# Begin the inverse with the score tiles, and put the panel split and the rotary angles ahead of it

## The reference, cut to what matters

```python
def step(state, inp):
    r_t, w_t, k_t, v_t, kk_t, a_t = inp
    sa = jnp.einsum('bhvk,bhk->bhv', state, -kk_t)
    state = (state * w_t[:, :, None, :] + sa[..., None] * (kk_t * a_t)[:, :, None, :]
             + v_t[..., None] * k_t[:, :, None, :])
    return state, jnp.einsum('bhvk,bhk->bhv', state, r_t)
```

## Time and profile before

| what | value |
|---|---|
| median of 3 runs | 1281.81 us (1281.0 to 1282.97) |
| the profiled execution | 1281.0 us, its span 1278.7 us |
| TensorE busy | 1133.4 us, 89% of the span |
| VectorE busy | 642.2 us, 50% |
| ScalarE busy | 467.8 us, 37% |
| mean granted TensorE clock | 0.959 |

### The profile page before, as it was taken

The page is one execution under the profiler, slowest core; times in us unless marked ns, Lnnn a source line. Parts: engine busy times, 40 slices in busy tenths (PEclk is TensorE's granted clock), DMA queues, the critical chain, the costliest instruction groups (busy, mean ns, idle before and its releaser), DMA issues.

```text
span 1278.7 us, 18185 instructions
## 1 busy us (share of the span) xinstructions
PE 1133.4 (89%) x7641; PEld 911.9 (71%) x7641; DVE 642.2 (50%) x899; ACT 467.8 (37%) x566; POOL 24.8 (2%) x43
## 2 busy tenths in 40 slices
PE   2599999999999989699688988795999999999985
PEld 2588757778887677587466766584888888878864
DVE  4867556355343456953853537635453333342334
ACT  4422441323323446555335655316312222232222
POOL 0100000000000000000000001000000000000000
PEclk9999989999999889899889999897999999999988
DMA  7866423311014331137031144722353322222201
GB/s 265 260 217 223 146 82 100 111 44 43 19 44 152 129 124 56 45 108 266 8 114 41 45 144 157 256 84 83 132 165 99 99 99 90 96 78 99 99 1 66
DMA packets 105401, 143.40 MB, mean 112 GB/s; under 512 B 3028, under 2 KB 86088, under 8 KB 105320
## 3 DMA queue, kind: packets, MB, share of 16 engines
q1 hardware_dynamic: 91816, 105.76, 25.3%
q0 software_dynamic: 6016, 22.84, 5.1%
q10 hardware_dynamic: 7488, 13.63, 2.9%
HBM read 126.50 MB, written 15.73 MB: 111 GB/s over the span
## 4 chain that ended last, share of the span: by engine, by line
PE 70%; DVE 16%; ACT 10%; issue 2%; DMA 1%; ACTq 0%; DVEq 0%; SPq 0%; POOL 0%
PE bank L1804 69%; DVE wlo L1175 2%; ACT whi L764 2%; DVE ada_acc L1178 2%; DVE mg L1175 1%; DMA raw<-in_ada_w 1%; ACT gate_row L779 1%; DVE q_lev L1175 1%; DVE Z L1175 1%; ACT sg L1131 1%; DVE near L1585 1%; DVE k_lev L1175 1%; DVE x L1175 1%; ACT x_norm L792 1%; ACT LX L887 1%
## 5 line engine op out<-in xcount | busy, mean ns | idle before, releaser
L1804 PE MATMUL bank<-hhi,whi 128*128 128x512 f32 x816 | 333.1, 408 | 11.8 <-DVE wlo L1175 8.9
L1175 DVE TENSOR_TENSOR wlo<-raw,whi 128x2048 fp32r<-128x2048 f32 (+1 forms) x82 | 175.2, 2136 | 333.8 <-ACT whi L764 333.1
L1804 PE MATMUL bank<-hlo,whi 128*128 128x512 f32 x816 | 323.3, 396 | 0.0
L1804 PE MATMUL bank<-hhi,wlo 128*128 128x512 f32 x816 | 322.8, 396 | 0.0
L764 ACT ACTIVATE whi<-raw 128x2048 fp32r<-128x2048 f32 (+1 forms) x82 | 146.9, 1792 | 220.7 <-PE bank L1804 205.0
L1804 PEld LDWEIGHTS bank<-hhi,whi 128*128 128x128 f32 x816 | 156.7, 192 | 55.4 <-DVE wlo L1175 9.6
L1804 PEld LDWEIGHTS bank<-hhi,wlo 128*128 128x128 f32 x816 | 156.4, 192 | 34.2
L1804 PEld LDWEIGHTS bank<-hlo,whi 128*128 128x128 f32 x816 | 157.1, 193 | 31.5 <-issue 0.5
L1804 PE MATMUL bank<-whi,d_hi 128*128 128x512 f32 x176 | 70.4, 400 | 7.7 <-DVE d_lo L1175 7.7
L1804 PE MATMUL bank<-wlo,d_hi 128*128 128x512 f32 x176 | 70.0, 398 | 0.0
L1804 PE MATMUL bank<-whi,d_lo 128*128 128x512 f32 x176 | 69.9, 397 | 0.0
(11 more groups left out here) (314 smaller groups left out, 1543.4 us busy)
## 6 DMA issues: line engine op xcount, KB each, us to landing
raw<-in_w_in SPq DMA_DIRECT2D x33, 1024.0 KB, 5.5
raw<-in_ada_w SPq DMA_DIRECT2D x24, 1024.0 KB, 5.2
raw<-in_f_in SPq DMA_DIRECT2D x22, 1024.0 KB, 5.1
early_out<-gate_row ACTq DMA_DIRECT2D x52, 256.0 KB, 2.0
raw<-in_f_out SPq DMA_DIRECT2D x11, 1024.0 KB, 4.9
sg<-early_out POOLq DMA_DIRECT2D x4, 1536.0 KB, 9.8
raw<-in_w_out SPq DMA_DIRECT2D x4, 1024.0 KB, 8.3
x_in<-in_x POOLq DMA_DIRECT2D x4, 512.0 KB, 7.9
```

Of the source, the lines that this page charges most:

```text
L1175: return v.tensor_tensor(out_, a, b, op)
L1804: return t.matmul(out_, lhsT, rhs, start=start, stop=stop, skip_group_check=True)
```

## The change

TensorE computes the four "rw sc" tiles before the two "rw n" tiles, and the bank plan adds them in that order. ScalarE takes "rw n" after early("rw pro") and after early(("rw lo", c)) instead of before. VectorE runs early("rw pro") ahead of begin_inverse(0), and in the rounds begin_inverse(c + 1) after the angles and the dot products instead of before them.

```diff
     def inverse_start(n):
         b.add("rw v", n)
-        for g in range(2):
-            b.add("rw n", n, g)
         for ab in range(2):
             for g in range(2):
                 b.add("rw sc", n, ab, g)
+        for g in range(2):
+            b.add("rw n", n, g)
...
             take_values(0)
+            early("rw pro")
             take_first(0)
-            early("rw pro")
...
                 take_values(c + 1)
+                early(("rw lo", c))
                 take_first(c + 1)
-                early(("rw lo", c))
                 take_r(c, 0)
...
+            early("rw pro")
             begin_inverse(0)
-            early("rw pro")
...
             for c in range(PAIRS - 1):
-                begin_inverse(c + 1)
                 if c == 0:
                     angles(1)
                 elif c == 1:
...
+                begin_inverse(c + 1)
                 early(("rw lo", c))
...
                 end(last, "rw v", n)
+                for ab in range(2):
+                    ps = [begin("rw sc", n, ab, g) for g in range(2)]
+                    for hl in range(4):
+                        for g in range(2):
+                            last = mm(ps[g][:, P * hl:P * hl + P], rows64(BK, g, hl, 2 * n + ab), rows64(AR, g, hl, 2 * n + ab))
+                            if hl == 3:
+                                end(last, "rw sc", n, ab, g)
                 ps = [begin("rw n", n, g) for g in range(2)]
...
-                for ab in range(2):
-                    ps = [begin("rw sc", n, ab, g) for g in range(2)]
...
```

## The result

The changed kernel took 1301.13 us (median of 4 runs, 1297.88 to 1302.47) against 1281.85 us for the kernel before (4 runs, 1281.0 to 1282.97). The ratio is 1.0146, interval 1.0125 to 1.0168. It was timed again later: 1302.88 against 1281.42 us, ratio 1.0157 (1.0137 to 1.0177). The forecast was 1304.2 us, slower by 22.4; measured was 19.3 and, the second time, 21.5 slower. The profiled execution of the changed kernel took 1297.93 us, at the lower end of its runs.

What follows compares the result with a forecast made beforehand. TensorE was taken to bound the kernel, so its stalls add to the end time. 8.2 + 3.8 + 3.8 + 0 + 6.6 = +22.4 us on the 1281.81 us median gave 1304.2 us; range 1296.5 to 1308.5.

Steps and rivals of the forecast that it cites:

- The wait of n for the masks: Ahead of the rounds n waits for VectorE's masks, +8.2 us; rounds 0 and 1, behind angles, +3.8 us net each.
- That the bank is the cause: In the inverse's start, n takes banks of the first two sc tiles, so it waits until VectorE masks them.
- the wait moves to `X`: Rival: n's bank is free, TensorE stops only at level 1; +10.3 us in all, 1292.1 us, chance 0.06.
- What the rounds get back: Rounds 0 and 1: TensorE's wait for `X` at level 1 goes, giving back 0.7 us of 4.5 in each.
- Round 2: Last inverse begun, no angles ahead of the masks: cost 0, up to 1.9 us if ScalarE's cover were gone.
- The clock: Behind each of three TensorE gaps, ahead of the rounds and in rounds 0 and 1: 2.2 us, 6.6 in all.
- stalls without the clock: Rival: the same three gaps come but the clock costs nothing; +15.8 us, 1297.6 us, chance 0.10.
- Sum: Whole kernel: 8.2 + 3.8 + 3.8 + 0 + 6.6 = +22.4 us, 1304.2 us.
- the shift at the stage's end stays to the end of the kernel: Profile sign: about 22 us later at the end of the stage, unchanged to the end of the kernel.
- Given back entirely: Rival: the stage ends later, but what it delays waits for something else anyway; 1281.8 us, chance 0.04.
- faster: Rival: in all four places masks start up to 1.0 us sooner, removing TensorE waits; -4.7 us, 1277.1 us, chance 0.05.

Runs made afterwards that it cites:

- TensorE's order alone: Kernel before with only TensorE's order and the bank plan changed, sc ahead of n; 1282.27 us (1.0004).
- gaps filled: Changed kernel plus matmuls nobody reads between sc and n, 32 ahead of the rounds, 17 in each of rounds 0 and 1; 1296.88 us (1.0113).
- TensorE undone: Changed kernel with TensorE's order and the bank plan as before, VectorE's and ScalarE's moves kept; 1296.06 us (1.0111).
- version to beat both: Kernel before with angles between levels 3 and 4, values in their own bank, and ScalarE copying n before the values; 1277.68 us (0.9969).
- n in other banks: Changed kernel with the two n tiles in banks 4 and 5, which VectorE need not free; 1289.92 us (1.0062).
- VectorE undone: Changed kernel with both of VectorE's edits taken back, TensorE's and ScalarE's kept; 1278.13 us (0.9978).
- angles undone: Changed kernel with begin_inverse(c + 1) ahead of the angles again in the rounds; 1288.12 us (1.0048).
- angles in the middle: Kernel before with only the angles and lambda moved between levels 3 and 4; 1277.85 us (0.9979).
- first begin undone: Changed kernel with VectorE running begin_inverse(0) before early("rw pro") again; 1287.88 us (1.0050).

## Why the prediction was right

- *The wait of n for the masks.* Right in mechanism and size. Ahead of the rounds I had 8.1 to 8.2 us; the run with filled gaps has 7.8 without the clock. In the rounds I had 3.8 net; 3.7 each. The gaps were 7.69, 4.38 and 4.42 us. The 0.4 us too much ahead of the rounds is ScalarE: its second store took 0.33 us in the queue, and the high half started at 231.40, not 231.83.
- *That the bank is the cause* was argued from the bank plan; giving n other banks showed it. The rival "the wait moves to `X`", priced at 5.1, 1.5 and 1.5 us and 2.2 for the clock behind the first, is what that kernel does: 7.5, 1.5 and 1.5, less 0.4 in round 2.
- *What the rounds get back.* I said that the wait for `X` is there once; it is there in rounds 0 and 1, 1.4 us in all, and was priced in both. I let the two waits go because the angles move. They go by TensorE's order alone as well, as three runs show; the number was right, the credit too narrow.
- *Round 2.* 0 forecast, -0.4 measured. The reason for no cost held: `LX` is copied by 374.63, and VectorE comes to it at 375.18.
- *The clock.* 2.2 us for each gap forecast, 6.6 in all; 2.7, 2.3 and 2.1 in the first profile, 1.5, 1.7 and 1.7 in the second. The rival "stalls without the clock" fell: filling the gaps took 6.7 us out of the stage. So the size was right in the first profile, and 1.6 us too high in the second; which of the two an execution gets was not foreseeable from the rows. By the 0.62, 0.67 and 0.71 above, 8 us x 2 x (1 - clock) is 6.1, 5.3 and 4.6 us at half clock. The Trainium skill (TensorE: Matmul & The Clock Gate, Terms) puts the penalty at the throttled time times (1 - K/N), half of it at half clock; that would be an estimate of 3.0, 2.6 and 2.3 us. The runs have 0.2 to 0.3 us less in each.
- *Sum.* +22.4 forecast, +22.0 and +19.8 in the stage, +19.3 and +21.5 in the medians. The term that was missing is outside the stage: I said that the shift at the stage's end stays to the end of the kernel, and 5.0 and 1.8 us of it came back behind it as the clock fell for less time there. That was neither priced nor in the range's reasoning. That the second difference of the medians comes within 1 us of the forecast is in part luck: in its profile 2.1 us less than in the first in the stage and 1.8 given back stand against 3.9 us lost ahead of the stage, which the edit doesn't touch.
- *Given back entirely* and *faster* fell with the result. The latter's mechanism was real, though: with VectorE's edits undone the rest of the change is worth 1.6 us in the stage.

What comes back behind the stage is the clock's. The 13 profiles differ in how long it stands at half around two places there, 421 and 462 us in the kernel before (read in windows of 0.2 us), and the time from the stage's end to the end of the kernel follows it:

| at half clock at the two places | profiles | from the stage's end to the last instruction |
|---|---|---|
| 13.6 us | kernel before (both), gaps filled, TensorE undone, version to beat both | 895.7 to 896.6 us |
| 10.2 us | changed kernel (second), n in other banks, VectorE undone | 894.3 to 894.8 us |
| 6.8 us | angles undone, TensorE's order alone, angles in the middle | 893.3 to 893.6 us |
| 3.4 us | changed kernel (first), first begin undone | 891.6 us |

Open: what decides between these. It is not the length of the stage, since versions with a longer and with a shorter one stand in the same row; the kernel before shows the same stretches twice and the changed kernel does not, and no run separates a cause in the order of the program from chance.

## What to carry to other kernels

When tiles share banks in rotation, exchanging two of them also exchanges whose reader they wait for; look up who frees the bank, and what stands ahead of that release in its reader's queue. Here, 5.5 us of angles moved ahead of a release made waits of 4.4 us, and each of these cost 1.7 to 2.3 us more by the clock. Place such work where its engine is idle anyway: the same angles between two levels made the stage 1.2 us shorter.

## What the runs showed of the hardware

The granted clock also falls where TensorE has no gap. In the kernel before it is 1.00 from 418.6 to 421.8 us, 0.51 from 421.8 to 428.8, which is 6.8 us at half, and 1.00 behind that. TensorE is busy all the time; just before the fall it works through matmuls that use 8 of the 128 rows (here the second line of TensorE's timeline; with the two behind it they last to 422.7). Whether these matmuls are the cause no run tests:

```profile
415.13 3.59 PE L1804 MATMUL bank<-AR,cst 128*128 128x512 f32 x8
418.66 2.84 PE L1804 MATMUL bank<-bonus,cst 8*128 8x512 f32 x6
```

Whether and how long it falls at this place differed between kernels with the same work there, 0, 3.4 or 6.8 us, and between the two profiles of the changed kernel, 0 and 3.4. It differs even ahead of the stage, where all the kernels are the same: those at half clock for 6.8 or 10.2 us in all reach the stage at 227.8 to 228.1 us (the kernel before and the changed kernel's first profile among them), those with 13.6 or 17.1 us at 230.6 to 231.9. So two profiles can differ by up to 4 us ahead of the stage and 5 us behind it without an edit that explains it; against that a measure of the stage alone is the sharper one.
